# A two-block layer kernel on one core: places of weight pieces and slots of landed weights, 16 bytes further apart each

## What is computed

```python
for i in range(2):                       # first block, x of [1, 256, 1024]
    h = h + 0.5 * rms_norm(swiglu(rms_norm(h, g[0]), ffn_w1[i, 0], ffn_w2[i, 0]), g[1])
    u = rms_norm(h, g[2])
    m = conv_ssd_mixer(u, ...) if i % 2 == 0 else dilated_attention_mixer(u, ...)
    h = h + rms_norm(m, g[3])
    h = h + 0.5 * rms_norm(swiglu(rms_norm(h, g[4]), ffn_w1[i, 1], ffn_w2[i, 1]), g[5])
h = layer_norm_2(h, ln_in_g, ln_in_b)    # second block
for layer in range(2):
    proj = h @ w_in[layer]               # [256, 1024] @ [1024, 11,776]
    y_a, y_b, y_c = retention(...) @ ret_w_out, hgrn2_scan(...) @ hgrn_w_out, swa_with_sinks(...) @ swa_w_out
    mix = (sigmoid(ga) * y_a + sigmoid(gb) * y_b + sigmoid(gc) * y_c) @ w_o[layer]
    h = layer_norm_2(DN_ALPHA * h + mix, ...)
    ff = swiglu_2(h, ...) if layer % 2 == 0 else moe_swiglu(h, ...)   # 8 experts, top 2, width 3584
    h = layer_norm_2(DN_ALPHA * h + ff, ...)
```

## Time and profile before

| | |
|---|---|
| median of 3 runs | 3175.64 us |
| lowest and highest | 3175.43 and 3178.93 us |
| profiled execution, first to last instruction | 3172.4 us |
| TensorE busy | 3136.1 us |
| VectorE busy | 2219.9 us |
| ScalarE busy | 1871.5 us |
| weights moved, all queues | 730.39 MB |

### The profile page before, as it was taken

The page is one execution under the profiler, slowest core; times in us unless marked ns, Lnnn a source line. Parts: engine busy times, 40 slices in busy tenths (PEclk is TensorE's granted clock), DMA queues, the critical chain, the costliest instruction groups (busy, mean ns, idle before and its releaser), DMA issues.

```text
span 3172.4 us, 39857 instructions
## 1 busy us (share of the span) xinstructions
PE 3136.1 (99%) x15857; PEld 2611.5 (82%) x15857; DVE 2219.9 (70%) x2626; ACT 1871.5 (59%) x2487; POOL 48.8 (2%) x67
## 2 busy tenths in 40 slices
PE   9999999999999999999999999999999999999998
PEld 7888588888887878988888889887888888888887
DVE  5559865655445566665754757667999999999998
ACT  5442554544455444655544457465777777777777
POOL 1000000000000000000000000000000000000000
PEclk9999999999999999999999999999999999999999
DMA  9444274665536444535374545346999999999995
GB/s 326 145 168 145 92 234 150 201 204 166 140 107 219 146 160 160 186 134 185 124 235 138 181 161 194 123 153 226 384 376 382 382 376 382 382 376 382 381 377 225
DMA packets 383079, 730.39 MB, mean 230 GB/s; under 512 B 13027, under 2 KB 152689, under 8 KB 382784
## 3 DMA queue, kind: packets, MB, share of 16 engines
q1 hardware_dynamic: 376576, 705.87, 62.4%
q0 software_dynamic: 6224, 22.16, 2.3%
q10 hardware_dynamic: 112, 0.05, 0.0%
HBM read 720.16 MB, written 7.86 MB: 229 GB/s over the span
## 4 chain that ended last, share of the span: by engine, by line
PE 93%; DVE 4%; ACT 2%; issue 0%; DMA 0%; DVEq 0%; SPq 0%; ACTq 0%
PE duo L1075 14%; PE duo L1077 14%; PE duo L1076 14%; PE acc L1075 8%; PE acc L1077 8%; PE acc L1076 8%; PE aux L1075 2%; PE aux L1076 2%; PE aux L1077 2%; PE aux L553 1%; PE duo L554 1%; PE duo L553 1%; PE aux L554 1%; PE duo L555 1%; PE aux L555 1%; PE duo L398 1%
## 5 line engine op out<-in xcount | busy, mean ns | idle before, releaser
L1741 DVE TENSOR_TENSOR weights_split<-w,weights_split 128x1024 fp32r<-128x1024 f32 x672 | 792.5, 1221 | 80.2 <-ACT weights_split L1717 78.9
L1717 ACT ACTIVATE weights_split<-w 128x1024 fp32r<-128x1024 f32 x672 | 675.3, 1053 | 205.4 <-PE duo L1077 128.3
L1075 PE MATMUL duo<-weights_split,u_high 128*128 128x512 f32 x1776 | 698.7, 393 | 1.2 <-issue 0.8
L1077 PE MATMUL duo<-weights_split,u_low 128*128 128x512 f32 x1776 | 692.6, 390 | 0.0
L1076 PE MATMUL duo<-weights_split,u_high 128*128 128x512 f32 x1776 | 692.0, 390 | 0.0
L427 DVE TENSOR_TENSOR w_low<-w,w_high 128x1024 fp32r<-128x1024 f32 x304 | 368.2, 1223 | 291.0 <-ACT w_high L418 289.6
L1220 DVE TENSOR_TENSOR weights_split<-w,weights_split 128x1024 fp32r<-128x1024 f32 x320 | 377.2, 1221 | 268.4 <-ACT weights_split L1208 268.2
L418 ACT ACTIVATE w_high<-w 128x1024 fp32r<-128x1024 f32 x304 | 318.2, 1057 | 315.1 <-PE acc L1077 80.2
L1208 ACT ACTIVATE weights_split<-w 128x1024 fp32r<-128x1024 f32 x320 | 320.7, 1054 | 239.3 <-PE duo L1077 139.9
L1075 PEld LDWEIGHTS duo<-weights_split,u_high 128*128 128x128 f32 x1776 | 333.7, 188 | 71.6 <-issue 3.7
L1077 PEld LDWEIGHTS duo<-weights_split,u_low 128*128 128x128 f32 x1776 | 333.5, 188 | 70.2
(11 more groups left out here) (448 smaller groups left out, 4954.8 us busy)
## 6 DMA issues: line engine op xcount, KB each, us to landing
w<-in_ffn_w_dram SPq DMA_DIRECT2D x130, 1024.0 KB, 7.8
w<-in_moe_w_gate_dram SPq DMA_DIRECT2D x112, 1024.0 KB, 8.1
w<-in_moe_w_up_dram SPq DMA_DIRECT2D x112, 1024.0 KB, 7.9
w<-in_moe_w_down_dram SPq DMA_DIRECT2D x112, 1024.0 KB, 9.6
w<-in_w_in_dram SPq DMA_DIRECT2D x92, 1024.0 KB, 7.2
w<-in_hyb_w_in_dram SPq DMA_DIRECT2D x18, 1024.0 KB, 8.2
w<-in_ffn_w_gate_dram SPq DMA_DIRECT2D x11, 1024.0 KB, 7.6
w<-in_ffn_w_up_dram SPq DMA_DIRECT2D x11, 1024.0 KB, 10.1
```

Source lines behind the costliest of these rows:

```text
L1075: pe.matmul(bank_out, x_hi, w_hi, start=first, stop=False, skip_group_check=True)
L1077: return pe.matmul(bank_out, x_lo, w_hi, start=False, stop=last, skip_group_check=True)
L1717: act.activation(units[:, place, 0, cut], src[:, cut], ACT.Copy).then_inc(sem("moe_high"), 1)
L1741: m = dve.tensor_tensor(units[:, place, 1, cut], src[:, cut], units[:, place, 0, cut], ALU.subtract)
```

## The change

Each slot of w1 and w_low becomes 4100 floats long, of which the first 4096 are used, and each place of w_high 1028, of which the first 1024 are used. The tiles "lead" and "gap" are gone. So slot s begins 16s bytes later than before, and place p of w_high 16p bytes later. The first slot, the first place, w2 and all tiles behind w_high begin where they began, since four times 16 bytes are the 64 bytes that each of the two tiles took. Every place in the code that takes a whole slot or a whole place now names its used part. The instructions of every engine, their order, sizes and waits are the same as before, so no order of instructions is shown.

```diff
@@ -158,14 +158,13 @@
 
 
 
-        with nc.sbuf_tensor("w1", [P, RING, 4096], F32) as w1:
+        SLOT, PIECE = 4096 + 4, 1024 + 4
+        with nc.sbuf_tensor("w1", [P, RING, SLOT], F32) as w1:
             pass
-        w_low = sb("w1_low", [P, RING, 4096], F32R)
-        sb("lead", [P, 16])
+        w_low = sb("w1_low", [P, RING, SLOT], F32R)
         with nc.sbuf_tensor("w2", [P, RING2, 2, D], F32) as w2:
             pass
-        w_high = sb("w2_high", [P, PIECES, 1024], F32R)
-        sb("gap", [P, 16])
+        w_high = sb("w2_high", [P, PIECES, PIECE], F32R)
         h = sb("h", [P, NT, D])
         u = sb("u", [P, KC, T])
         rows = sb("rows", [P, 2, D])
@@ -310,7 +309,7 @@
             n = ring_pe["w1"]
             ring_pe["w1"] += 1
...
-                slot = w1[:, n1 % RING, :].rearrange("p (t n) -> p t n", n=COLS)
+                slot = w1[:, n1 % RING, 0:4096].rearrange("p (t n) -> p t n", n=COLS)
...
-                act.activation(w_high[:, q % PIECES, :], w1[:, n % RING, 1024 * p:1024 * (p + 1)], ACT.Copy)\
+                act.activation(w_high[:, q % PIECES, 0:1024], w1[:, n % RING, 1024 * p:1024 * (p + 1)], ACT.Copy)\
...
-            return w_high[:, q % PIECES, :], w_low[:, n % RING, 1024 * p:1024 * (p + 1)]
+            return w_high[:, q % PIECES, 0:1024], w_low[:, n % RING, 1024 * p:1024 * (p + 1)]
...
```

## The result

The changed kernel takes 3181.94 us (median of 18 runs), the kernel before 3174.55 us (18 runs beside them). One of the 18 took 7671.72 us, for a reason that nothing here shows, and the ratio leaves it out; the other 17 took 3179.89 to 3186.94 us. The ratio is 1.0022, with a 95% interval from 1.0015 to 1.003: **7.4 us slower**. It lies inside the range that was given, but only since the range was drawn wide enough to take in the rival C; the case that I took for the likeliest, no effect, is not what happened. The profiled execution of after spans 3181.4 us, 9.0 more than that of before.

A forecast was written before the change was run, and what follows sets the result against it. TensorE's row of matmuls was taken to bound the kernel. ScalarE/VectorE, DMAs and PE's pace summed as 0 + 0 + 0 on the 3175.6 us median, giving 3176 us, range 3161 to 3190.

The forecast's parts named there:

- rival C: Stages fed in pieces, 190 to 2180 us: unequal tile positions cause the excess, shifts slow the pace; 10.9 us, 3187; chance 0.24.
- no effect: Whole kernel: the change leaves the time at 3176 us, some 3 us to each side; chance 0.47.
- What bounds the kernel: Whole kernel: TensorE, busy 3136.1 of 3172.4 us; layout acts only through matmul pace or a feeder that makes PE wait.
- the excess: Matmuls on pieces: slower than the 226.6 ns pace of unmoved tiles, together 10.7 to 16.1 us, 0.3 to 0.5% of the span.
- Part 1, ScalarE and VectorE: Copies and subtractions on shifted tiles: costed at nothing, since PE covers up to 10% more VectorE time in the last stage.
- Part 2, the DMAs: Weight loads into shifted slots, expert stage: costed at nothing; half the packets may get 11% longer before PE waits.
- Rival D: DMAs into slots 1 and 3: packets take half as long again, over 100 us more; chance 0.05.
- The estimate of 1.6% more beats: DMA packets to shifted slots: a 2048-byte run starting at an odd 16 takes 65 beats, not 64; would change nothing.
- Part 3, PE's pace: Matmuls on high and low pieces: change of pace taken as 0, between ends of -16 and +16 us; the deciding term.
- the excess goes by groups of tiles and not by place: Rows of matmuls on moving pieces: starts go on evenly while places change, taken as evidence against an effect.
- the edge of the sweep and not its middle: PE's operand streams: a start 16 to 48 bytes later changes only the edge, argued for 0.
- Rival B: Matmuls on pieces: equal or near positions cause the excess, spreading takes half or all, 8 to 16 us; chance 0.24.

## Why the prediction was right or wrong

- **What bounds the kernel**, right: PE's row of matmuls is the time, the pace and not the duration shows it, and the layout acts through the pace on pieces alone. But the excess (10.7 to 16.1 us) only bounds what a layout can gain, not what it can cost: the experiments moved the time from 4.9 us below before to 11 us above, and the upper bound of the range had no better ground than two levels of the rows.
- **Part 1, ScalarE and VectorE at nothing**, right: the medians of after are those of the earlier trace rows within 1 ns.
- **Part 2, the DMAs at nothing**, right: landings and waits as in the earlier trace rows. Rival D is out. The estimate of 1.6% more beats from the Trainium skill (DMA: Bandwidth & Descriptors, "How a descriptor splits into AXI transactions") can't be seen in landings of 9.6, 8.0 and 8.0 us. It isn't refuted either: the queue still waits for free slots (566.4 us at L1907), so the transfers don't set the time.
- **Part 3, PE's pace at 0 between -16 and +16**, wrong, and this is the step that failed. By the delay of the same matmul it is 7.9 us over 4752 matmuls, 1.7 ns each; by the averages of all groups 1.7 ns on each stationary matmul (352.9 against 347.8 a group) and 1.8 on each moving one (696.3 against 690.8). The sentence that failed is "the excess goes by groups of tiles and not by place: the earlier trace rows run through all four places". The observation was true; the conclusion wasn't. In the kernel before, the places lie 4096 bytes apart and the slots 16384, all at one position modulo 256. Its rows had no variation in position in them, and so could say nothing on what a variation costs. And "the edge of the sweep and not its middle" is refuted by the run with the low pieces 16 bytes later: every group costs 5.6 ns more for it. That the measured time still lies in the range is owed to the range and not to this step: the value was 0, and only the bound taken from one more step of the rows covers it.
- **Rival C** had the mechanism and the sign: "the excess comes from tiles standing at different positions", with starts within 64 bytes adding something. Its price of 10.9 us was too high by 3.0 for the change. Its description was too simple as well: with everything at position 0 the moving pieces do run at the full pace, but the stationary ones are the slowest of all (120.0 ns), and the best pair for them (64, 192) isn't an equal one.
- **Rival B**, the gain, is open in this direction and closed in the change's own: other positions do take excess away, but spreading them over four didn't.
- **The sentence on the Trainium skill** (SBUF — State Buffer, "Who interferes with whom"), by which PE never waits on anyone and the shift is worth 0: the trace disagrees with the 0. The sentence of that page is about engines that wait for one another, and no run here shows PE waiting so; what fails is the step from it to a pace that can't depend on positions. 347.8 became 352.8, 353.4 or 341.7 ns a group, by a shift of tiles and nothing else. Leaving 0 as the value while noting that the rule didn't explain the 226.6 against 231.2 ns of the earlier trace rows was the inconsistency; an unexplained excess on just the moved tiles deserved more weight than a rule that couldn't account for it.
- **The sum against the profiled execution**: of the 9.0 us between the spans, 7.9 are pace and 2.6 PE at the lower clock level at 2195 to 2215 us, less 1.2 that the kernel before loses to its own such stretch near 805 us and 0.3 at the start. No term stood for the clock. It isn't a cost of this change, as far as the runs tell: at equal mean clock the kernels differ by 7.5 us. Whether a layout can change how often the clock falls is open: with the high pieces 16 bytes later 10 of 11 runs have a mean clock of 0.998, where 23 of the 28 runs of before beside them have 0.999.

What stays open: which part of the machine makes the pace go by the positions of the two operands, and why the first moving piece behind a step is slow from its first group to its last, with a distance of 261 ns in many of its second groups. The runs show the dependence and its sizes; they don't show the cause.

## What to carry to other kernels

Where long rows of matmuls run at slightly different paces from different tiles (here 226.6 and 231.2 ns for the same shape), the start of the tiles modulo 256 bytes is a parameter that is worth a few runs: stationary and moving operands want different positions, and a well chosen pair for all buffers of a ring beats a spread (3169.5 against 3181.94 us), while a badly chosen one doesn't (3184.63). The gain is small, 0.14 to 0.17% here. Evidence that a quantity doesn't matter needs rows in which it varies; a ring whose slots are all alike modulo 256 has none. A wait that takes one piece of lead from ScalarE let PE stand still for 3 us more at a single place here: look up who runs with the least lead before costing such a wait. And before two profiles are subtracted, look the same matmul up in both all along the way: here the difference of the spans held 1.4 us of PE's clock.

## What was unexpected

- The distance of two matmuls from start to start goes by where the operands start: 226.8 to 233.3 ns for 512 columns and 113.8 to 120.0 for 256, with the instructions, waits and DMAs the same. 16 bytes are enough: 347.8 against 353.4 ns a group.
- The pair of positions that is best for moving pieces (0, 0) is the worst for stationary ones, of the pairs that were measured.
- A piece whose place starts 16 bytes after that of the one before it is slower in all its four groups (2.84 us for 2.76 in all), while the next one at the same position isn't.
- Spreading both rings cost less (7.4 us) than spreading the places alone (10.9; 7.5 and 9.8 at equal clock); the two intervals overlap, but the averages of all groups say the same of the moving pieces (696.3 and 699.4 ns).
- PE's granted clock falls to the lower level for 3.4 us here and there when PE had gaps (at routing, or at the turn of a stage): 0.83 over a stretch of 10 us. It stands at other places in other profiles. Two such stretches cost after 2.6 us in its profile, and one costs before 1.2.
